# Two routers, two expert stages and the joints between them: router logits in column groups, the first gather inside the router's stage, the down bias added per expert

## The reference

```python
# block 1
x = x + g1 * hybrid_mixer(h)                      # gated delta rule and SSD heads, then w_out
h = rmsnorm(x, norm2_g) * (1 + sc2) + sh2
logits = h @ router_w + router_b                  # 32 experts, the 4 largest kept, softmax over them
y_e = swiglu(x_rows @ w_gu[e] + b_gu[e]) @ w_down[e] + b_down[e]     # 1024 -> 2048 -> 1024
x = x + g2 * sum over a token's experts of gate * y_e
x = rmsnorm(x, final_g)
# block 2
u = rms_norm(x, g_mix); z = u @ w_in_2            # sparse attention with compressed blocks, and GLA
x = x + mixed(z) @ w_out_2
v = rms_norm(x, g_ffn)
# 4 groups of 8 experts: softmax over groups, the best group, in it the best 2
y_e = (silu(v @ w_gate[e]) * (v @ w_up[e])) @ w_down[e]              # 1024 -> 512 -> 1024
out = rms_norm(x + sum of gate * y_e, g_final)
```

## Time and profile before

| | us |
|---|---|
| median of 3 runs (2229.11 to 2230.7) | 2229.33 |
| the profiled execution | 2227.41 |
| its span, first to last instruction | 2225.7 |
| TensorE busy in the span | 2078.5 (93%) |
| mean granted TensorE clock | 0.978 of 2.4 GHz |

### The profile page before, as it was taken

The page is one execution under the profiler, slowest core; times in us unless marked ns, Lnnn a source line. Parts: engine busy times, 40 slices in busy tenths (PEclk is TensorE's granted clock), DMA queues, the critical chain, the costliest instruction groups (busy, mean ns, idle before and its releaser), DMA issues. The chain is left out here.

```text
span 2225.7 us, 25010 instructions
## 1 busy us (share of the span) xinstructions
PE 2078.5 (93%) x10093; PEld 1056.0 (47%) x10093; DVE 547.9 (25%) x1154; ACT 368.4 (17%) x626; POOL 97.7 (4%) x171
## 2 busy tenths in 40 slices
PE   3999999989999999999999999799899899999998
PEld 1768676654444433333334333355464444444443
DVE  1436543442222211221122212322342200000001
ACT  2133431210000000000000000213341111111112
POOL 0101042010000000000000000100030000000000
PEclk7999999989999999999999999899999899999999
DMA  9233163559999999999999999834253499999995
GB/s 334 95 123 114 38 240 115 209 204 427 428 428 429 428 428 429 428 428 428 429 429 428 429 428 429 309 114 164 60 189 150 180 428 429 429 428 428 429 429 243
DMA packets 98749, 708.59 MB, mean 318 GB/s; under 512 B 12306, under 2 KB 17900, under 8 KB 61580
## 3 DMA queue, kind: packets, MB, share of 16 engines
q1 hardware_dynamic: 98700, 707.92, 77.3%
HBM read 706.85 MB, written 1.05 MB: 318 GB/s over the span
## 5 line engine op out<-in xcount | busy, mean ns | idle before, releaser
L1584 PE MATMUL ps<-ring,arena 128*64 128x512 f32 x2048 | 452.0, 594 | 28.5 <-DMA ring<-in_moe_w_gu 28.5
L1584 PEld LDWEIGHTS ps<-ring,arena 128*64 128x64 f32 x2048 | 161.2, 137 | 312.9 <-issue 247.3
L1606 PE MATMUL ps<-ring,arena 128*64 128x512 f32 x1024 | 226.8, 594 | 19.6 <-issue 19.6
L2750 PE MATMUL ps<-ring,arena 128*64 128x512 f32 x1024 | 224.7, 593 | 6.7 <-DMA ring<-in_w_up 5.3
L1606 PEld LDWEIGHTS ps<-ring,arena 128*64 128x64 f32 x1024 | 84.6, 137 | 141.2 <-issue 141.2
L2750 PEld LDWEIGHTS ps<-ring,arena 128*64 128x64 f32 x1024 | 77.9, 137 | 150.3 <-issue 150.3
L1637 ACT ACTIVATE arena<-arena 128x512 f32<-128x512 f32 x32 | 20.1, 630 | 767.9 <-DVE arena L1683 767.9
L2021 PE MATMUL ps<-ring 128*128 128x512 f32 (+1 forms) x320 | 139.9, 587 | 1.4 <-DVE ring L2483 0.8
L2771 PE MATMUL ps<-ring,arena 128*64 128x512 f32 x512 | 113.4, 595 | 0.0
L1683 DVE TENSOR_SCALAR arena<-ps 128x512 f32<-128x512 f32 x32 | 22.1, 691 | 332.3 <-PE ps L1584 332.3
L2811 DVE TENSOR_SCALAR arena<-iota_row,arena 128x64 f32<-128x64 f32 x68 | 12.6, 249 | 326.8 <-PE ps L2750 325.3
(11 more groups left out here) (561 smaller groups left out, 2064.8 us busy)
## 6 DMA issues: line engine op xcount, KB each, us to landing
ring<-in_moe_w_gu SPq DMA_DIRECT2D x128, 2048.0 KB, 24.1
ring<-in_moe_w_down SPq DMA_DIRECT2D x64, 2048.0 KB, 21.4
ring<-in_w_down SPq DMA_DIRECT2D x32, 2048.0 KB, 12.1
ring<-in_w_gate SPq DMA_DIRECT2D x32, 2048.0 KB, 14.8
ring<-in_w_up SPq DMA_DIRECT2D x32, 2048.0 KB, 17.2
ring<-in_w_in SPq DMA_DIRECT2D x22, 2048.0 KB, 11.5
ring<-in_ada_w SPq DMA_DIRECT2D x12, 2048.0 KB, 10.2
ring<-in_w_out SPq DMA_DIRECT2D x6, 2048.0 KB, 8.4
```

Of the source, the lines that this page charges most:

```text
L1584: last = M.matmul(ps[halves[j], 4 + which, :], xgT[buf][:, k, CAP * ee:CAP * ee + CAP], w[:, k2, at:at + 512], start=False, stop=(k == KD ...
L1606: last = M.matmul(ps[halves[j], 6, :], yT[:, k % KH, halves[k // KH]], w[:, k % KH, 512 * j:512 * j + 512], start=(k == 0), stop=(k == 2 * ...
L2750: last = M.matmul(ps[halves[j], 4 + which, :], xgT[:, k, halves[j]], w[j][:, k, :], start=(k == 0), stop=(k == KD - 1))
```

## The change

- The router's weights become the stationary operand, in column groups: eight k slices spread over four groups of 32 columns in the first router, over two groups of 64 (36 padded with zeros) in the second. The partial sums go through an ACT copy (`lgp`, `lgp2`) and are folded by one matmul with `pick` or `fold2`.
- `pick`, `quarter` and `fold2` are made once by POOL in an early block, beside its masks.
- `start_from_residual` moves ahead, between transposes and logits. In the second router ACT squares both tiles before it copies the first transposes, DVE multiplies by `fgn` ahead of the root, and `select_first` replaces `select_top` for the group.
- `dispatch_tables` is split into `first_slots` and `pass_count`; the first one-hot and the first gather, the clearing of `y2` and `GT` and the first bias selector come into the router's block.
- The down bias enters each expert's bank 6 through its bias selector (`bias_dn`) ahead of the down product; the product after the loop, `gT` and the multiplication of `bdn` go. The selector has two buffers.
- `bias_dn` and the four transfers of `pos_rows` are issued by SP at the head of the first experts' block.
- In the second mixer the first projection unit waits for the two copies of tile 0 alone, the second unit for those of tile 1. POOL clears the padded router weights before they are loaded.

```diff
+            gg(G.tensor_tensor(pick[:, 0:32], ident[:, 0:32], ident[:, 32:64], ALU.add))
+            gg(G.tensor_tensor(pick[:, 0:32], pick[:, 0:32], ident[:, 64:96], ALU.add))
+            gg(G.tensor_tensor(pick[:, 0:32], pick[:, 0:32], ident[:, 96:128], ALU.add))
+            gg(G.tensor_copy(pick[:, 32:36], pick[:, 0:4]))
+            gg(G.tensor_tensor(fold2, ident[:, 0:36], ident[:, 64:100], ALU.add))
+            for g in range(4):
+                gg(G.memset(quarter[:, g:g + 1], 0.0))
+                gg(G.memset(quarter[32 * g:32 * g + 32, g:g + 1], 1.0))
...
+    def first_slots(dve, rank_bank, s_rank, s_slot):
 
         dve.wait_ge(s_rank, 1)
         V.scalar_tensor_tensor(tmp2, ps[:, rank_bank, 0:64].rearrange("p (t e) -> p t e", t=T), 1.0, sel,
                                ALU.add, ALU.mult).then_inc(s_slot, 1)
         dve.wait_ge(s_slot, 1)
+        vv(V.tensor_scalar(slot_of[:, :, 0:NE], tmp2, -1.0, None, ALU.add))
+
+    def pass_count(rank_bank):
+
         vv(V.tensor_reduce(cmax[:, 0:1], ps[:, rank_bank, 64:96], X_AXIS, ALU.max))
-        vv(V.tensor_scalar(slot_of[:, :, 0:NE], tmp2, -1.0, None, ALU.add))
         vv(V.tensor_scalar(cmax[:, 1:2], cmax[:, 0:1], float(CAP), 1.0, ALU.is_gt, ALU.add))
         for b in range(2, MAXP):
             vv(V.scalar_tensor_tensor(cmax[:, 1:2], cmax[:, 0:1], float(b * CAP), cmax[:, 1:2], ALU.is_gt, ALU.add))
         vv(V.tensor_copy(passes[0:1, 0:1], cmax[0:1, 1:2]))
...
+    def select_first(l, m8, sel, tmp):
+
+        n = l.shape[1]
+        vv(V.max(m8, l))
+        vv(V.tensor_scalar(tmp, l, m8[:, 0:1], None, ALU.is_equal))
+        cum = scratch_cum[:, 0:n]
+        vv(V.tensor_tensor_scan(cum, ones[:, 0:n], tmp, 0.0, ALU.mult, ALU.add))
+        vv(V.scalar_tensor_tensor(sel, cum, 1.0, tmp, ALU.is_le, ALU.mult))
...
-            sp.wait_ge(s_o, 1)
-            sp.dma_start(bdn[0:NE, :], a["moe_b_down"][0]).then_inc(s_bdn, 16)
...
+            def partial_logits(t):
+                for r in range(2):
+                    pe.wait_ge(s_h2Tt, 2 * t + r + 1)
+                    for g in range(4):
+                        last = M.matmul(ps[32 * g:32 * g + 32, 4 + 2 * t, 0:P], rw[:, 4 * r + g, :], h2T[:, 4 * r + g, toks(t)],
+                                        start=(r == 0), stop=(r == 1))
+                last.then_inc(s_lp, 1)
+
             def router_logits(t):
-                pe.wait_ge(s_res, 3 + t)
-                for k in range(KD):
-                    if k % 4 == 0:
-                        pe.wait_ge(s_h2Tt, 2 * t + k // 4 + 1)
-                    last = M.matmul(ps[:, 4 + t, 0:NE], h2T[:, k, toks(t)], rw[:, k, :], start=(k == 0), stop=(k == KD - 1))
-                last.then_inc(s_lg, 1)
+                pe.wait_ge(s_lpt, t + 1)
+                M.matmul(ps[:, 5 + 2 * t, 0:NE], lgp[:, t, :], pick[:, 0:NE]).then_inc(s_lg, 1)
 
             normed_transposes(0)
+            start_from_residual(0)
             pe.wait_ge(s_n2, 48)
+            pe.wait_ge(s_res, 4)
+            partial_logits(0)
+            start_from_residual(1)
+            normed_transposes(1)
             router_logits(0)
-            normed_transposes(1)
+            partial_logits(1)
+            router_logits(1)
             pe.wait_ge(s_nm, 1)
             first_ranks(4)
-            router_logits(1)
-            start_from_residual(0)
             pe.wait_ge(s_nm, 2)
             second_ranks(4).then_inc(s_rk, 1)
-            start_from_residual(1)
+            pe.wait_ge(s_one1, 1)
+            for half in range(2):
+                gather_half(h2, onehot1, half, 6 + half, s_xg1)
...
+                act.wait_ge(s_lp, t + 1)
+                A.activation(lgp[:, t, :], ps[:, 4 + 2 * t, 0:P], ACT.Copy).then_inc(s_lpt, 1)
...
+            first_slots(dve, 4, s_rk, s_slot1)
+            dve.wait_ge(s_iota, 1)
+            make_onehot(onehot1, first_slot_of, 0, s_one1)
...
-            dispatch_tables(dve, 4, s_rk, s_slot1)
...
+            pass_count(4)
+            V.memset(y21, 0.0).then_inc(s_y21, 1)
+            V.memset(GT1, 0.0).then_inc(s_GTt1, 1)
+            V.tensor_scalar(bsel1[0], bcast(quarter, CAP), pick[:, 0:1], None, ALU.mult).then_inc(s_bs1, 1)
...
+                for j in range(2):
+                    sp.dma_start(bias_dn[32 * j:32 * j + 32, :], a["moe_b_down"][0][:, 512 * j:512 * j + 512]).then_inc(s_bdn, 16)
+                for i, kv in enumerate("kv"):
+                    sp.dma_start(pos_rows[16 * i:16 * i + 16, :], a[f"cmp_pos_{kv}_2"][0].rearrange("(j i) d -> j (i d)", i=2)).then_inc(s_p9, 16)
+                    sp.dma_start(pos_rows[32 + 2 * i:34 + 2 * i, :], a[f"cmp_b1_{kv}_2"][0].rearrange("(k p) -> k p", p=P)).then_inc(s_p9, 16)
...
+                G.memset(bias_dn[halves[1], :], 0.0).then_inc(s_b64, 1)
+                gg(G.tensor_copy(g2s[halves[0], :], mods[halves[0], 3, 0:512]))
+                G.tensor_copy(g2s[halves[1], :], mods[halves[1], 3, 512:1024]).then_inc(s_g2, 1)
...
-                for t in range(T):
-                    last = M.transpose(ps[0:NE, 5, t * P:(t + 1) * P], gate_of[:, t, 0:NE], ident[:, :])
-                last.then_inc(s_gT, 1)
-                pe.wait_ge(s_one, 1)
-                for half in range(2):
-                    gather_half(half, 6 + half)
                 pe.wait_ge(s_bgu, 64)
-                pe.wait_ge(s_gTt, 1)
...
+                            if u == 0:
+                                pe.wait_ge(s_bdn, 32)
+                                pe.wait_ge(s_b64, 1)
+                            for j in range(2):
+                                M.matmul(ps[halves[j], 6, :], bsel[ee][:, j, :], bias_dn, start=True, stop=False)
                             pe.wait_ge(s_yTt, i + 1)
...
-                                                    start=(k == 0), stop=(k == 2 * KH - 1))
+                                                    start=False, stop=(k == 2 * KH - 1))
...
-                pe.wait_ge(s_g2, 1)
-                for t in range(T):
-                    for d in range(2):
-                        M.matmul(ps[:, 2 * t + d, :], gT[0:NE, t * P:(t + 1) * P], bdn[0:NE, 512 * d:512 * d + 512],
-                                 start=False, stop=False, skip_group_check=True)
...
-                make_onehot(0)
-                V.memset(y2, 0.0).then_inc(s_y2, 1)
-                V.memset(GT, 0.0).then_inc(s_GTt, 1)
-                vv(V.tensor_tensor(pick[:, 0:32], ident[:, 0:32], ident[:, 32:64], ALU.add))
-                vv(V.tensor_tensor(pick[:, 0:32], pick[:, 0:32], ident[:, 64:96], ALU.add))
-                vv(V.tensor_tensor(pick[:, 0:32], pick[:, 0:32], ident[:, 96:128], ALU.add))
-                vv(V.tensor_copy(pick[:, 32:36], pick[:, 0:4]))
-                vv(V.tensor_reduce(quarter, ident[:, :].rearrange("p (g e) -> p g e", g=4), X_AXIS, ALU.add))
-                select_bias(0)
...
-            for i, kv in enumerate("kv"):
-                sp.dma_start(pos_rows[16 * i:16 * i + 16, :], a[f"cmp_pos_{kv}_2"][0].rearrange("(j i) d -> j (i d)", i=2)).then_inc(s_p9, 16)
-                sp.dma_start(pos_rows[32 + 2 * i:34 + 2 * i, :], a[f"cmp_b1_{kv}_2"][0].rearrange("(k p) -> k p", p=P)).then_inc(s_p9, 16)
...
-            sp.wait_ge(s_kct, 1)
+            sp.wait_ge(s_rwz, 1)
...
+            pool.wait_ge(s_kct, 1)
+            G.memset(rw2, 0.0).then_inc(s_rwz, 1)
...
-            pe.wait_ge(s_uTt, 4)
+            pe.wait_ge(s_uTd, 2)
             for u in range(FIRST):
                 j, t = divmod(u, 2)
+                if u == 1:
+                    pe.wait_ge(s_uTt, 2)
...
+            def partial_logits(t):
+                for r in range(4):
+                    if r % 2 == 0:
+                        pe.wait_ge(s_nTt, 2 * t + r // 2 + 1)
+                    for j in range(2):
+                        last = M.matmul(ps[halves[j], 4 + 2 * t, 0:P], rw2[:, 2 * r + j, :], h2bT[:, 2 * r + j, t * P:(t + 1) * P],
+                                        start=(r == 0), stop=(r == 3))
+                last.then_inc(s_lp2, 1)
+
             def router_logits(t):
-                pe.wait_ge(s_nTt, t + 1)
-                for k in range(KD):
-                    last = M.matmul(ps[:, (2, 7)[t], 0:36], h2bT[:, k, t * P:(t + 1) * P], rw2[:, k, :],
-                                    start=(k == 0), stop=(k == KD - 1))
-                last.then_inc(s_l11, 1)
+                pe.wait_ge(s_lpt2, t + 1)
+                M.matmul(ps[:, 5 + 2 * t, 0:36], lgp2[:, t, :], fold2).then_inc(s_l11, 1)
...
             transpose_normed(0)
+            start_from_residual(0)
             pe.wait_ge(s_p11, 80)
+            partial_logits(0)
+            pe.wait_ge(s_r11, 2)
+            start_from_residual(1)
+            transpose_normed(1)
             router_logits(0)
-            transpose_normed(1)
+            partial_logits(1)
             router_logits(1)
-            start_from_residual(0)
             pe.wait_ge(s_m11, 1)
-            first_ranks(6)
```

(31 more changed lines are left out.)

141 lines of the change are left out of this document (67 added, 74 removed).

## The result

The changed kernel takes 2208.03 us (median of 4 runs, 2205.64 to 2209.12) against 2229.22 for the kernel before (2227.81 to 2230.7): ratio 0.9903, 95% interval 0.9886 to 0.9921. The forecast was 2214.2, range 2208.5 to 2223.0. On two other chips the same pair gave 0.9919 (0.9905 to 0.9932) and 0.9911 (0.9896 to 0.9926), so the gain is 18 to 21 us where 15.1 were forecast. The profiled execution took 2207.94, and its span fell from 2225.7 to 2206.2.

The account below looks back on a forecast made before the run. Weight transfers were taken to bound the expert stages and TensorE the second mixer, so the joints count: 3.7 + 2.4 + 5.1 + 3.9 = 15.1 us, from 2229.33 to 2214.2 us, range 2208.5 to 2223.

Parts of the forecast that it names:

- First router: From the first router to the first expert weights: routes run back to back, gather inside the router, weights 3.7 us earlier.
- Loop and its end: First expert loop: added bias costs about 0.4 us in the last turn, last scatter 2.78 earlier; net 2.4 us gained.
- rival (c): First loop: the added bias makes TensorE the bound in each turn, up to 2244.0 us at 2.2 a turn; chance 0.04.
- what exceeds 1.24 us, 31 times: First loop: price of added TensorE work, only the part above 1.24 us of slack a turn counting, over 31 turns.
- Start of the second mixer: Second mixer's projections no longer wait for `pos_rows`, starting 8.05 us earlier, 2.4 already counted; net 5.1 us (1.0 to 5.6).
- Rival (b): Second mixer: projections wait for something other than `pos_rows` and the copies, leaving 1.0 of 5.1 us; 2218.3; chance 0.12.
- Second router: Second router to the pairs' first weights: shorter routes run back to back, L2750 at 1743.8 instead of 1747.77; 3.9 us.
- the start of its projections decides: Second mixer, slices 26 to 30: TensorE busy nine tenths, transfers slack, so only when projections start was taken to matter.
- The median of the runs stands 1.92 above: Whole kernel: the runs' median was taken 1.92 us above the profiled execution, raising 2212.3 to the predicted 2214.2.
- (a): Both routers and second mixer's projections: TensorE idles and half clock lasts beyond the gathers; 2225.0 us; chance 0.15, whole or part.
- (d): Both routers: both gathers run at full clock, gaining 18.1 us in all, to 2211.2; chance 0.14.
- (e): Expert stages: the first refill does not start the weight stream, so the routers give nothing; 2221.8 us; chance 0.03.

Follow-up runs that it names:

- tripled bias: Against the changed kernel, the down bias product is entered three times over in each turn of the first loop; 2232.94 us (one execution).
- late rows: Against the changed kernel, the four position-row transfers are issued at the head of the second mixer again; 2214.05 us, ratio 0.9943 to the kernel before.
- the fillers: Against the changed kernel, identity products nobody reads in TensorE's waits, both routers and second mixer's start; 2203.94 us (ratio 0.9892), 2202.82 (0.9894) on another chip.

## Why the prediction was right in its parts and too small in its sum

The forecast of 2214.2 stands 6.2 above the measured 2208.03. Of that 4.4 us are in the span of the profiles, and 1.8 in the step from the profile to the median.

**First router, 3.7 forecast, 4.19 measured.** Less the 0.74 of the later start, the steps stand at 471.26 (forecast 471.3), tile 0 routed 474.23 (474.6), routes over 478.83 (479.3), gather 481.27 (481.5), weights 490.30 (490.8). That the partial sums end where they should is luck: they took 0.82 instead of 0.5, but started before the second copy was done. The gather took 5.45 where 5.36 was chosen. The runs say what carries the gain: the early gather 3.8, the column groups 1.3 and what they spare in half clock. Undone singly these come to more than 4.19, since each also lengthens the stretch at half clock. The queue order was not undone by itself.

**Loop and its end, 2.4 forecast, 2.47 measured.** The last slot comes 3.71 earlier than before (1402.86 to 1399.15) and the block 6.18. The added bias was mis-sized on the safe side, 0.17 a turn for 0.36 to 0.97, so rival (c) fell. Its mechanism is real, but its price was put too low: with the tripled bias, 1.89 a turn more than before, the rule "what exceeds 1.24 us, 31 times" gives 20.2, and the loop up to the projections took 25.75 longer than in the changed kernel (963.86 against 938.11). The slack was 1.50, not the wait of 1.24; but once every turn is above 29.36, the early turns that waited for nothing cost their full length as well.

**Start of the second mixer, 5.1 forecast, 5.04 measured**: 5.82 up to the projections, less 0.78 for half clock in their first 80 instructions (0.5 was allowed). Rival (b) fell: nothing stood behind `pos_rows` but `un` and its copies, and with late rows 5.89 of it went again.

**Second router, 3.9 forecast, 4.22 measured.** The route fell to 3.84 (3.95 forecast), the gather took 5.59 (5.36). The early gather carries 3.4 of it; the column groups and the shorter route were not undone here.

**The step that failed** is in the first part: in the second mixer "the start of its projections decides". That took the 277 us between the projections and the norm's transposes as fixed, and gave them neither a term nor a share of the range. They are not fixed. In the execution that was shown the kernel before had half clock there: 2.78 more in the output projections, and 1.40 more ahead of them, of which 0.84 in the projection behind a wait of 4.7 (5.71 against 4.87) and 0.54 in the narrow products. The same program spends this or not. Between the two profiles shown it was 4.18 of the 4.4 us that the span's gain exceeded the forecast by; the four terms together exceed it by 0.8 (15.92 against 15.1), the loop's transfers add 0.26, and the start of the program and the pairs give 0.86 back. A second, smaller step: "The median of the runs stands 1.92 above" the profile was carried over as if it were a property of the kernel, while the changed kernel's stands 0.09 above its own.

Over four profiles before and three after, the mean span falls by 17.2 (2224.6 to 2207.4), 2.1 more than the forecast. The middle of the second mixer has 0.9 of that, the second router 1.1 (5.0 against 3.9): where the kernel before kept the clock in the mixer, its second router lost more. So that the two profiles shown differ by 19.5 is in part chance, the choice of the execution. All executions, 40 of the kernel before with a mean of 2227.4 and thirteen of the changed one with 2208.1, differ by 19.3. The 2.1 between the two figures was not traced to a place and stays open.

**The other rivals.** (a) *Half clock takes the gain*: at the gathers as the sum had it, not beyond; the first weights run at 1.00 in both stages. The Trainium skill, "TensorE: Matmul & The Clock Gate", part 1, says that activity brings the clock back from 1.2 to 2.4 GHz, and also that how many matmuls run slow at a kernel's start differs from run to run of one kernel. The first agrees here: the filled gathers take 3.84 at 1.00. The second the page says of the start alone; here the output projections of one program, far behind the start, took 3.70 or 6.48. (d) *Gathers at full clock* did not come of itself, though the time is below even its 2211.2; the fillers brought it. (e) *Hidden anyway* fell: the first refill went out 3.44 earlier, and the loop's last slot 3.71.

## What to carry to other kernels

A stage whose instructions do not change is not a stage whose time does not change: take several profiles of the kernel before, and give each stretch where the granted clock can fall a share of the range. Where TensorE waits for another engine on the path, what it does in the wait sets the price of the work behind it, and products that nobody reads were worth 4.3 us here. Slack of an engine is read from a turn that waits for nothing, not from the wait that the profile shows.

## What the runs showed of the hardware

The clock fell to 0.5 while TensorE was busy without a gap, but with products of 16 columns (L2226 before, L2269 after, 64 instructions in 3.77 to 4.86 us), in three of 17 profiles. With one and the same program, executions spread over 6 us (2205.64 to 2212.02), and the shorter ones mostly have the higher mean clock (0.986 for the shortest, 0.982 for the longest). The wait for the four transfers of `pos_rows` varied in the kernel before: from the loop's end to the projections the kernel before took 13.65 to 16.76 in four profiles, the changed one 10.96 in all three.
